# First layer of a two-layer decoder on one Trainium2 core: the projection's products run 24 matmuls ahead of their periods, and the value convolution moves with them

## What is computed

```python
proj = rmsnorm(x) @ w_in                      # columns: q, k, v, z (1024 each) and two gates
qkv  = silu(causal_depthwise_conv(proj_qkv))  # 4 taps along the tokens
q, k = l2norm(q) * D**-0.5, l2norm(k)         # 8 heads of 128
# chunked gated delta rule, per head: a triangular solve per chunk, then a scan over chunks
sol  = triangular_solve(I + strict(kb k^T * decay), [vb, kb * exp(g)])
for i in chunks: v_new = u_i - w_i S;  o_i = qg_i S + a_i v_new;  S = S*gl_i + kt_i^T v_new
x    = x + (rmsnorm(o) * silu(z)) @ w_out
```

## Time and profile before

| | us |
|---|---|
| median of 3 runs | 1309.57 (1309.38 to 1310.67) |
| the profiled execution | 1308.67 |
| its span, first to last instruction | 1306.7 |
| period -1 | 75.3 to 131.9 |
| period 0 | 131.9 to 199.3 |
| periods 1 to 5 | 69.6 to 69.9 each |
| period 6 | 548.3 to 613.6 |
| period 7 | 613.6 to 674.3 |

### The profile page before, as it was taken

The page is one execution under the profiler, slowest core; times in us unless marked ns, Lnnn a source line. Parts: engine busy times, 40 slices in busy tenths (PEclk is TensorE's granted clock), DMA queues, the critical chain, the costliest instruction groups (busy, mean ns, idle before and its releaser), DMA issues.

```text
span 1306.7 us, 18255 instructions
## 1 busy us (share of the span) xinstructions
PE 1257.5 (96%) x6701; PEld 1047.9 (80%) x6701; DVE 947.2 (72%) x1749; ACT 704.8 (54%) x1185; POOL 587.8 (45%) x380
## 2 busy tenths in 40 slices
PE   6998999999999999999997999999999999998997
PEld 5777788888888888878886778888888888886786
DVE  5587888888788888883349768787877777786313
ACT  6354456464656364643336665666665666665203
POOL 6533353443434333432128685656647375622400
PEclk9999999999999999999998999999999999999999
DMA  7311111201111110234225021211111111228503
GB/s 189 87 35 31 33 49 34 61 21 49 49 49 49 49 49 25 65 130 147 72 56 181 6 59 30 75 49 49 50 49 49 49 49 49 81 61 278 178 1 129
DMA packets 106858, 91.42 MB, mean 70 GB/s; under 512 B 3105, under 2 KB 92306, under 8 KB 106770
## 3 DMA queue, kind: packets, MB, share of 16 engines
q1 hardware_dynamic: 106770, 90.25, 22.9%
HBM read 66.65 MB, written 23.59 MB: 69 GB/s over the span
## 4 chain that ended last, share of the span: by engine, by line
PE 73%; DVE 13%; ACT 6%; issue 3%; POOL 3%; DMA 1%; DVEq 0%; SPq 0%; ACTq 0%; POOLq 0%
PE psum L532 23%; PE psum L698 19%; PE psum L712 5%; PE psum L2585 5%; DVE late L1839 3%; PE psum L2559 3%; PE psum L2572 2%; PE psum L2469 2%; PE psum L671 2%; DVE late L1836 2%; PE psum L2490 2%; DVE stick L2154 1%; PE psum L2500 1%; ACT late L1357 1%; PE psum L2423 1%
## 5 line engine op out<-in xcount | busy, mean ns | idle before, releaser
L532 PE MATMUL psum<-u_hi,w_hi 128*128 128x512 f32 x640 | 260.0, 406 | 4.2 <-DVE u_lo L1693 1.7
L532 PE MATMUL psum<-u_hi,w_lo 128*128 128x512 f32 x640 | 258.6, 404 | 0.0
L532 PE MATMUL psum<-u_lo,w_hi 128*128 128x512 f32 x640 | 257.3, 402 | 0.0
L499 POOL TENSOR_TENSOR w_lo<-w_raw,w_hi 128x1024 fp32r<-128x1024 f32 (+1 forms) x45 | 107.8, 2394 | 249.9 <-ACT w_hi L494 237.7
L532 PEld LDWEIGHTS psum<-u_hi,w_hi 128*128 128x128 f32 x640 | 120.9, 189 | 29.1 <-issue 4.2
L532 PEld LDWEIGHTS psum<-u_hi,w_lo 128*128 128x128 f32 x640 | 120.8, 189 | 23.4 <-issue 1.7
L532 PEld LDWEIGHTS psum<-u_lo,w_hi 128*128 128x128 f32 x640 | 121.1, 189 | 20.8 <-issue 0.5
L1839 DVE SCALAR_TENSOR_TENSOR late<-raw,cols,late 128x1024 f32<-128x1024 f32 x72 | 120.3, 1671 | 1.8
L640 POOL TENSOR_TENSOR w_lo<-w_raw_b,w_hi 128x512 fp32r<-128x512 f32 x40 | 58.3, 1459 | 110.9 <-ACT w_hi L624 110.9
L2154 DVE TENSOR_TENSOR_SCAN stick<-soft 128x1024 f32<-128x1024 f32 (+3 forms) x64 | 104.1, 1627 | 0.2
L698 PE MATMUL psum<-u_hi,w_hi 128*128 128x512 f32 x240 | 95.9, 399 | 0.5
(11 more groups left out here) (308 smaller groups left out, 3200.8 us busy)
## 6 DMA issues: line engine op xcount, KB each, us to landing
w_raw<-in_a_w_in SPq DMA_DIRECT2D x33, 512.0 KB, 4.2
w_raw<-in_b_w_in SPq DMA_DIRECT2D x16, 512.0 KB, 5.5
w_raw_b<-in_b_w_in SPq DMA_DIRECT2D x16, 512.0 KB, 5.9
b_rows<-o_part SPq DMA_DIRECT2D x14, 512.0 KB, 3.8
o_rows<-o_part_a SPq DMA_DIRECT2D x12, 512.0 KB, 3.6
x_stage<-in_x SPq DMA_DIRECT2D x8, 512.0 KB, 7.4
out<-fin_o SPq DMA_DIRECT2D x8, 512.0 KB, 2.6
u_lo<-b_rows SPq DMA_DIRECT2D x7, 512.0 KB, 8.2
```

Source lines behind the costliest of these rows:

```text
L499: G.tensor_tensor(lo_tiles(key), raw_tiles(key), hi_tiles(key).bitcast(F32), ALU.subtract).then_inc(lo_done, 1)
L532: mm = PE.matmul(psum[:, half], (w_hi, w_hi, w_lo)[part][:, buffer(key), k], (u_hi, u_lo, u_hi)[part][:, k, half * HALF:(half + 1) * HALF] ...
```

## The change

All products of layer 0's fill run 24 (half a key) ahead: period -1 issues also the first half of ("z", 0), every later period starts with the second half of its z and ends with the first half of the next z, and period 7 issues 24 fewer. `FILL_FIRST` now sums to 168 (144 before). `SLOT_FILL`, `FILL_0` and `FILL_6` are as they were, `FILL_7` has one product less in each slot. A key thus ends 24 products earlier: z in slot 2 (before: 6), q in 8 (10), k in 13 (16), v in 20 (23). Takes and splits move along with it. Taps 8, 9 of v move from slot 0 of the next period to slot 22, tap 10 from slot 1 to slot 23, tap 11 from slot 1 to slot 0. Head 0's taps stay in period -1's slots 0 and 1.

```diff
-TAPS_AT = {0: (8, 9), 1: (10, 11), 13: (0,), 14: (1, 2), 16: (3,), 17: (4, 5), 19: (6, 7)}
+AHEAD = 24
+TAPS_FIRST = {0: (8, 9), 1: (10, 11)}
+TAPS_AT = {22: (8, 9), 23: (10,), 13: (0,), 14: (1, 2), 16: (3,), 17: (4, 5), 19: (6, 7)}
 SLOT_FILL = (6, 9, 11, 10, 2, 8, 10, 11, 11, 11, 10, 10, 9, 8, 6, 6, 8, 6, 6, 8, 6, 6, 6, 8)
-FILL_FIRST = (8, 8, 8, 7, 3, 7, 8, 9, 9, 9, 9, 8, 6, 5) + (4,) * 10
+FILL_FIRST = (8, 8, 9, 9, 5, 8, 9, 9, 10, 10, 9, 9, 6, 4, 3, 3, 7) + (6,) * 7
 FILL_0 = (16, 9, 9, 7, 2, 7, 9, 10, 10, 10, 10, 10, 9, 8, 6, 6, 8, 6, 6, 8, 6, 6, 6, 8)
 FILL_6 = (6, 9, 10, 8, 2, 8, 10, 9, 9, 9, 8, 8) + (6,) * 7 + (8, 6, 6, 6, 3)
-FILL_7 = (10,) + (9,) * 23
+FILL_7 = (9,) + (8,) * 23
...
-        FILLS = {-1: ([(part, 1) for part in "qkv"], 0, in_all(FILL_FIRST))}
+        FILLS = {-1: ([(part, 1) for part in "qkv"] + [("z", 0)], 0, in_all(FILL_FIRST))}
         for t in range(H - 2):
-            FILLS[t] = ([("z", t)] + [(part, t + 2) for part in "qkv"], 0, in_all(SLOT_FILL if t > 0 else FILL_0))
+            FILLS[t] = ([("z", t)] + [(part, t + 2) for part in "qkv"] + [("z", t + 1)], AHEAD,
+                        [AHEAD + n for n in in_all(SLOT_FILL if t > 0 else FILL_0)])
         ENDING = [("z", H - 2), ("z", H - 1)] + [("early", cb) for cb in range(KB)]
-        FILLS[H - 2] = (ENDING, 0, in_all(FILL_6))
-        FILLS[H - 1] = (ENDING, sum(FILL_6), [sum(FILL_6) + n for n in in_all(FILL_7)])
+        FILLS[H - 2] = (ENDING, AHEAD, [AHEAD + n for n in in_all(FILL_6)])
+        FILLS[H - 1] = (ENDING, AHEAD + sum(FILL_6), [AHEAD + sum(FILL_6) + n for n in in_all(FILL_7)])
...
-                    for tap_no in TAPS_AT.get(s, ()):
-                        h = t + (1 if tap_no >= 8 else 2)
-                        if h < H:
-                            conv_tap(h, tap_no)
+                    if t < 0:
+                        for tap_no in TAPS_FIRST.get(s, ()):
+                            conv_tap(0, tap_no)
+                    if s == 0 and 0 <= t < H - 1:
+                        conv_tap(t + 1, 11)
+                    if t + 2 < H:
+                        for tap_no in TAPS_AT.get(s, ()):
+                            conv_tap(t + 2, tap_no)
```

## The result

The changed kernel takes 1359.91 us (median of 4, 1358.09 to 1361.56) against 1309.47 us for the kernel before on the same chip: 1.0383 times as long, 95% interval 1.0365 to 1.0401. The prediction was 1360 us, range 1318 to 1374. The profiled execution took 1360.39 us.

A forecast was written before the change was run, and what follows sets the result against it. The prediction took the kernel as bound by PE, with DVE close behind. Its terms, -4.7 - 1.3 + 7.2 + 40.8 + 9.6 = +51.6 us on 1308.67, gave 1360 us, range 1318 to 1374.

The forecast's parts named there:

- Tails: Slots 20 to 23, six period ends: POOL blocks taps and square_lo, 5.1 us each plus half clock; +40.8 us, bounds 6 to 45.
- half clock: After each tail's idle PE runs at 1.2 GHz, losing 1.7 us; also expected gone in period -1, gaining 1.7 us.
- lower bound without collisions: Each tail: ACT's squares and v_new of slot 22 come 1.06 us later, and PE with them, +1.0 us.
- Slots 13 to 16: Tap 1 meets POOL's moved split, making invT and turn late; +1.2 us in periods 0 to 5, +7.2 us.
- Slots 0 to 7: Slot 4's wait goes, the split delays the mask, slot 7 waits; net +0.25 us in periods 1 to 5; sum -1.3 us.
- Products: 24 products leave period 7 and join period -1, whose half clock goes; -4.7 us, bounds -2.5 to -6.
- Period 6, rows read back: ("early", 0) starts 24 products earlier and waits for its rows: +7.9 us and 1.7 for the clock, +9.6 us.
- rival 1: Collisions cost little, about 1 us a tail, as DVE and POOL interleave; about 1325 us; chance 0.15.
- rival 3: Faster: DVE's slack at the period's end takes taps and square_lo, rhs waits go; 1295 us; chance of faster 0.11.
- Rival 2: Only part of the tail: square_lo isn't blocked or the clock holds; about 1344 us; chance 0.2.
- The signs: Profile after: 3 to 4 us idle before L2447, taps 2 to 3 us, period 3 78 us, waits in slots 7, 16.

The follow-up runs named there:

- experiment 1: The changed kernel with square_lo ahead of taps 8 and 9 in slot 22; 1338.95 us, ratio 1.0231.
- kernel 3: The changed kernel with only the weight split of slot 20 put back to slot 23 on ACT and POOL, periods 0 to 5; 1319.36 us, ratio 1.0089.
- experiment 4: On top of kernel 3, the split of slot 13 put back to slot 16 as well; 1312.62 us, one execution.
- kernel 6: On top of kernel 5, square_lo ahead of taps 8 and 9; 1306.60 us, ratio 0.9986.
- experiment 8: On top of kernel 6, rows 0 to 4 read back without waiting for row 5's store to land; 1305.13 us, ratio 0.9972.
- kernel 5: The changed kernel with all weight splits of periods 0 to 5 back in the earlier kernel's slots, taps left at the period's end; 1309.04 us, ratio 1.0002.
- experiment 10: On top of experiment 8, 12 products of slots 9 to 11 of period 6 moved to slots 14 to 23; 1304.84 us, ratio 0.9970.
- kernels 6 to 10: Kernel 6, 1306.60 us; only products ahead, 1312.76; experiment 8, 1305.13; that with 24 products moved from period 6 to 7, 1303.15; experiment 10, 1304.84.
- kernel 2: The changed kernel with v's taps 8 to 11 back in slots 0 and 1 of the next period; 1329.50 us, ratio 1.0165.

## Why the prediction was right, point by point

The time came out for the reasons given, with errors of single terms of up to 4.7 us that cancel; that it lies within 0.1 us of the median, where the four executions spread over 3.5 us, is luck.

- **Tails** (predicted +40.8): each has 4.26 us before L2454 and 0.72 us more before v_new than the 0.26 it had, together 4.98 against the 5.1 predicted; and 2.6 us of half clock, not 1.7. 7.6 x 6 is 45.5, above the bound of 45. The mis-sized term is the half clock: it was taken from one place, behind a wait of 2.69 us, and here it lasted longer (a dozen spacings of 0.43 us). The mechanism is shown by experiments 1 and 3: blocking by POOL, of `square_lo` too. The lower bound without collisions, 1.0 us for ACT's lateness, was about right: of it v_new costs 0.72 us here. DVE's order alone adds to it: kernel 3, where ACT isn't late, has 0.55 us idle before the period's first matmul.
- **Slots 13 to 16** (+7.2): 1.2 us a period as predicted (1.0 up to the start of `turn` and 0.2 behind it), +7.3; shown by experiment 4, where a period fell from 71.6 to 70.4 us. The two taps were 1.7 us late, `invT` 1.3.
- **Slots 0 to 7** (-1.3): slot 4's 0.95 went; slot 7's wait costs 0.70 to 0.80 a period instead of 1.2. So -0.25 instead of +0.25 in periods 1 to 5; with 2.2 us won in period 0 and 0.9 in period 6, -4.3. decT ended 13.9 us into a period that begins with 2.6 us of half clock (11.4 predicted), and the mask at 19.6 (17.5 predicted): the chain is the foreseen one, but DVE's queue behind the mask took up part of the delay.
- **Products** (-4.7): period 7 fell by 6.1 (predicted 6.2), period -1 rose by 2.5 instead of 1.5. The half clock there did go, as predicted (1.00 now, 0.72 in the earlier trace rows), the wait before `turn` is 0.84 us; two others, of 0.7 and 0.4 us, are new. Sum -3.7, within the bounds.
- **Period 6, rows read back** (+9.6): the waits for rows are 5.7 us (3.38, 1.19, 0.60 and 0.56 with their restarts), not 7.9, and the half clock about 1.4 instead of 1.7; +7.1. The waits were sized too long: 593.8 less 585.4 is 8.4 us, of which the prediction took 7.9. In kernels 3 and 6 they were 7.4 and 6.7 us, in kernel 3 without any half clock behind them. One cause was missed: DVE's take of z in slot 9 ends just ahead of row 0 (at 630.69, PE goes on at 631.02), so rows that come sooner gain little (experiment 8).
- **Rivals.** 1 and 3 needed POOL and DVE to pass each other cheaply; they don't. With POOL's splits elsewhere (kernel 5) the two taps and `square_lo` need 3.4 us, PE waits 0.53, the 5 us in slot 4 are won, and the change breaks even; what is left against rival 3 is the read-back, as it said. Rival 2 falls by the changed kernel's own trace, where the clock fell in all six tails, and by kernel 3, where `square_lo` takes 1.22 us once the sums are over, and not 2.91.
- **The signs** named ahead appeared: no wait in slot 4, one in slot 7, `turn` waiting in slot 16, a period of 78 us; the idle time of 4.1 us and tap 8's 1.94 us lie just outside the 3 to 4 and 2 to 3 us given. The terms as measured add up to 45.5 + 7.3 - 4.3 - 3.7 + 7.1 = 51.9, against the span's 51.7 us.

What stays open is why experiment 10 gained nothing, how the last 0.3 us in slots 0 and 1 of kernel 6 divide between taps and o_sq, and when the clock falls: the half clock behind the waits of period 6 differs from kernel to kernel, by more than some of the differences between kernels 6 to 10.

## What to carry to other kernels

When work is moved to run ahead, look at what is issued at its ends: here the 24 products cost and gave a few us, while the weight splits that are issued where a block ends slid two to five slots forward on two other engines and cost 50. Ask of every two large instructions on VectorE and GpSimd that a move brings together whether one waits for the whole of the other; the sum over such pairs, in the order of both queues, gave the stall within 3%, though one of them had never met in the trace. And issue an instruction by when its result is due, not by when its input is free: the splits had a whole block of products to spare.

## What the runs showed of the hardware

- 1024-wide two-input instructions of VectorE and GpSimd took turns, whole instruction by whole instruction: taps of 1.28 and `square_lo` of 1.22 us took 2.8 to 2.9 us each beside GpSimd's sums, and the two sums 5.19 instead of 3.75 us; all four together took 6.27 us, where the times alone add up to 6.25. A tap with one input (0.75 us) took 1.94 and 2.38 us, so it is held up as well.
- TensorE's granted clock: behind all six waits of 4.1 us matmuls ran on at 1.2 GHz (2.6 us lost each), and so they did behind 3.13 us in the changed kernel (about 1.4) and 2.69 us in the kernel before (1.7). The length of the wait alone doesn't settle it. Behind waits of 1.92 us in experiment 1 the clock fell in two cases of six, and behind 3.10 and 3.39 us for the rows in kernels 2 and 3 it didn't: there products went on at 0.23 us. The stretch behind the wait of 3.39 us (kernel 3, columns as in the earlier trace rows):

```profile
590.20:594.20 4.00, 2.63 (x13) 1.96 (x13) 1.23 (x8) 0.01 (x1) 0.00 (x0) 1.00 1.01 350
```
